# Two weight slabs in flight instead of three, and twelve places for gathered rows instead of eight

## What is computed

```python
s1 = jnp.einsum('thd,kd->thk', q[..., :half], keys_1)
s2 = jnp.einsum('thd,kd->thk', q[..., half:], keys_2)
...
act = jax.nn.gelu(jnp.einsum('td,tkd->tk', xt, peer_u[it]), approximate=False)
return jnp.einsum('tk,tkd->td', gt * act, peer_v[it])
```

## Time and profile before

| what | value |
|---|---|
| median of the 3 timed runs | 3032.58 us (3027.8 to 3038.06) |
| profiled execution, time | 3017.4 us |
| profiled execution, span from the first to the last instruction | 3016.1 us |
| PE busy | 2197.6 us, 73% |
| DVE busy | 1695.0 us, 56% |
| POOL busy | 1269.6 us, 42% |
| mean granted TensorE clock | 0.821 of full speed |
| moved by DMA | 829.54 MB, of it 539.99 MB gathered and 283.19 MB of slabs |

### The profile page before, as it was taken

How to read it: one execution, slowest core, us unless ns; L and a number is a source line. 1 busy time by engine, 2 the same in 40 slices (tenths; PEclk the granted TensorE clock), 3 DMA queues, 4 the chain that set the end, 5 groups by cost and what they waited for, 6 DMA issues and landing times. The chain is left out here.

```text
span 3016.1 us, 24315 instructions
## 1 busy us (share of the span) xinstructions
PE 2197.6 (73%) x8042; PEld 1333.1 (44%) x8042; DVE 1695.0 (56%) x3733; ACT 514.4 (17%) x1409; POOL 1269.6 (42%) x1041
## 2 busy tenths in 40 slices
PE   6997981155592594788682478979956598969988
PEld 3535861032342482433342247658423343436543
DVE  2512017968778767766577896765565854224200
ACT  1202000111210100122100452012001431004210
POOL 1000002466656666666666775664654633100000
PEclk9796996577595697899886558989978689988999
DMA  5210433698789899989889887999998879942466
GB/s 182 80 70 28 153 120 108 199 366 329 258 318 357 310 413 355 381 323 341 330 297 407 305 286 274 400 371 390 369 372 324 283 259 403 358 152 98 169 243 222
DMA packets 173485, 829.54 MB, mean 275 GB/s; under 512 B 20496, under 2 KB 21696, under 8 KB 155568
## 3 DMA queue, kind: packets, MB, share of 16 engines
q0 software_dynamic: 148464, 539.99, 48.9%
q1 hardware_dynamic: 21600, 283.19, 24.1%
q10 hardware_dynamic: 3296, 4.80, 0.5%
HBM read 825.81 MB, written 2.10 MB: 274 GB/s over the span
## 5 line engine op out<-in xcount | busy, mean ns | idle before, releaser
L326 POOL DMA_INDIRECT picks_rows<-peer_u_dram,expert x512 | 643.2, 1256 | 861.9 <-DVE expert L1545 481.2
L326 POOL DMA_INDIRECT picks_rows<-peer_v_dram,expert x512 | 618.5, 1208 | 479.5 <-DVE h L392 319.5
L386 DVE CUSTOM_DVE_ANT_0 picks_rows<-picks_rows,xn 128x1024 f32<-128x1024 f32 x512 | 611.5, 1222 | 184.5 <-DMA picks_rows<-peer_u_dram,expert 162.0
L392 DVE SCALAR_TENSOR_TENSOR h<-picks_rows,picks_weight,h 128x1024 f32<-128x1024 f32 x416 | 533.8, 1283 | 172.7 <-DMA picks_rows<-peer_v_dram,expert 98.2
L477 PE MATMUL psum<-weight_ring,hnT 128*128 128x512 f32 (+4 forms) x576 | 234.3, 568 | 15.5 <-DVE hnT L633 9.9
L1842 PE MATMUL psum<-weight_ring,aT 128*128 128x512 f32 x512 | 220.5, 593 | 2.3 <-ACT aT L2162 1.4
L415 PE MATMUL psum<-picks_rows,picks_diag 128*128 128x512 f32 x384 | 170.8, 605 | 19.1 <-ACT picks_diag L344 18.8
L477 PEld LDWEIGHTS psum<-weight_ring,hnT 128*128 128x128 f32 (+1 forms) x576 | 104.9, 184 | 143.8 <-issue 128.0
L1842 PEld LDWEIGHTS psum<-weight_ring,aT 128*128 128x128 f32 x512 | 97.0, 190 | 124.2 <-issue 121.0
L668 PE MATMUL psum<-identity_sb,n_scaled 128*128 128x128 f32 (+1 forms) x104 | 23.7, 408 | 157.1 <-DVE n_scaled L652 157.1
L477 PE MATMUL psum<-weight_ring,mergedT 128*128 128x512 f32 x256 | 115.9, 614 | 25.6 <-DVE mergedT L1267 24.2
(11 more groups left out here) (370 smaller groups left out, 2925.9 us busy)
## 6 DMA issues: line engine op xcount, KB each, us to landing
weight_ring<-slabs_dram SPq DMA_DIRECT2D x125, 2048.0 KB, 9.8
weight_ring<-slabs_dram SPq DMA_DIRECT2D x10, 1024.0 KB, 7.9
picks_rows<-peer_u_dram,expert POOLq DMA_INDIRECT x512, 7.2
picks_rows<-peer_v_dram,expert POOLq DMA_INDIRECT x512, 6.3
weight_ring<-slabs_dram SPq DMA_DIRECT2D x2, 1536.0 KB, 6.4
weight_ring<-slabs_dram SPq DMA_DIRECT2D x2, 1152.0 KB, 7.0
weight_ring<-slabs_dram SPq DMA_DIRECT2D x4, 576.0 KB, 5.9
weight_ring<-slabs_dram SPq DMA_DIRECT2D x4, 512.0 KB, 5.5
```

The source lines that it names most:

```text
L326: pool.indirect_dma_start(out=self.rows[:, n % GATHERS, :], out_offset=None, in_=table, in_offset=bass.IndirectOffsetOnAxis(ap=self.expert ...
L386: ins = nc.vector.tensor_tensor_reduce(out=row, in0=row, in1=self.x[t], scale=1.0, scalar=0.0, op0=ALU.mult, op1=ALU.add, accum_out=self.d ...
L392: ins = nc.vector.scalar_tensor_tensor(out=h, in0=row, scalar=self.weight[:, t % 2, k:k + 1], in1=h, op0=ALU.mult, op1=ALU.add)
```

## The change

The ring of weight slabs has two slabs instead of three, and its third slab's 16 KB per partition go to four more places for gathered rows, so that there are twelve. `cand_rest` no longer has memory of its own but lies in `scratch`.

```diff
-RING = 3
+RING = 2
 SLAB = KT * 512
...
-GATHERS = 8
+GATHERS = 12
 DIAGS = 8
...
         at_f = sb("at_f", [P, PH, 2, TOPK])
-        cand, cand_rest = sb("cand", [P, PH, N_SUMS]), sb("cand_rest", [P, PH, N_SUMS])
+        cand = sb("cand", [P, PH, N_SUMS])
+        cand_rest = scratch[:, 0:PH * N_SUMS].rearrange("p (h k) -> p h k", h=PH)
```

## The result

| | kernel before | changed kernel |
|---|---|---|
| median | 3030.93 us (3012.95 to 3042.47, 20 runs) | 3041.22 us (3026.99 to 3049.73, 20 runs) |
| span of the profiled execution | 3016.1 us | 3038.9 us |
| mean granted TensorE clock | 0.821 | 0.824 |

The ratio is 1.0038 [1.0025, 1.0051]: 11.5 us slower (7.6 to 15.5; the medians are 10.3 us apart), where +33 was forecast. The sign was right, the size was not. Repeated on a second chip the changed kernel stood at 1.0114 [1.0068, 1.0161], and on a third at 1.0035 [1.0015, 1.0054]. More on that under the last experiments.

The account below looks back on a forecast made before the run. DVE was taken as behind while picks run (502 to 2250 us), PE as the limit from 2250 us. Ring 78 us lost less places 45 gained is 33 more; scaled, 3032.6 x 1.011 = 3066 us, range 3005 to 3105.

Parts of the forecast that it names:

- "PE sets the pace" from 2250 us on: From 2250 us to the end PE is the limit, DVE and ACT only follow; the smaller ring costs most there.
- 38 - 7.4 + 23 = 54 us: Ring losses: 38 us from 2250 to 2650 us, 23 in the last run, without 7.4 at the compression.
- I count half, 14 us: Between 610 and 1950 us, two-tile runs: 28 us of slab waits on PE, half counted as loss, 14 us.
- The compression of the one-tile run: In the run from 2250 to 2650 us, first slab behind the branch gates: load 10.3 less cover 2.9, 7.4 us lost.
- "3 us" before 460 us: Three places behind 1024 KB slabs before 460 us, where PE is alone, about 1 us each: 3 us lost.
- The ring in all: Loss from two slabs instead of three, whole kernel: 3 + 14 + 38 + 23 = 78 us, between 50 and 110.
- The places: Gain from four more gathers under way or waiting, out of DVE's 260 us of waits: 45 us, bounds zero and 100.
- the stretch at a share of 0.97: 1050 to 1250 us, 46.0 us of DVE waits, DMA full: 8 us gained, only by what was filled ahead.
- the stretch from 1250: 1250 to 1500 us, 69.7 us of DVE waits at a DMA share of 0.90: 18 us gained.
- all outside the four rows: DVE waits outside the four listed stretches, 56 us in small pieces: 5 us gained.
- The clock "at nothing": New PE pauses of 1 to 7 us were taken to cost nothing through a lower PE clock afterwards.
- Rival C: Each PE pause also costs its clock, 2.5 us each: 34 us on the forecast, 3100 us; chance 0.15.

Follow-up runs that it names:

- the last experiments: The unedited changed kernel timed again on two other chips, against the kernel before: ratios 1.0114 and 1.0035 (3041.02 us).
- late2_g8: Kernel before (eight places, three slabs' memory), but slabs from 90 on take turns in two slots: 3095.54 us, ratio 1.0173.
- late_third: Changed kernel, but from pick 972 only eight places, the other four's memory being a third slab from slab 92 on: 2999.73 us, ratio 0.9848; again 0.9874.
- mid2_g8: Kernel before (eight places, three slabs' memory), but slabs 24 to 89 take turns in two slots: 3042.14 us, ratio 0.9996.
- both_third: As late_third, with the third slab for slabs 0 to 23 too: 3006.87 us, ratio 0.9899 to the kernel before; again 0.9862.
- early_back: Changed kernel, but twelve places only until pick 760, then eight, and the third slab back from slab 68 on: 2986.62 us, ratio 0.9868.

## Why the prediction was right in sign and wrong in size

- **"PE sets the pace" from 2250 us on, and each slab's price is landing less cover.** Right. 38 - 7.4 + 23 = 54 us forecast for the slabs from 90 on; late2_g8 lost 52 and late_third gave back 58. In the last run the waits of 4 to 5 us behind short slabs and 1.3 us between full ones are as worked out, and the loads of the last stretch land in 8.2 us, as in the earlier trace rows. The Trainium skill's fit beside the prices in the prediction (DMA: Bandwidth & Descriptors, anatomy of one DMA), 6.8 us for such a slab, is stated there for transfers that GpSimd issues. These loads come from SP, and the traces have 7.7 to 8.2 us.
- **"I count half, 14 us" for the waits between 610 and 1950 us.** This step failed. With the next one it makes up 21 of the 21.5 us by which the forecast was too high. The waits came (25.7 us, 22 of them new), but mid2_g8 shows their price as zero (its interval reaches to 5 us). The row beside which I counted half, PE's 16.99 us for `mergedT`, said it already: PE was early there by more than the merge's slabs could cost it.
- **The compression of the one-tile run, 7.4 of the 38 us.** The same fault. I took all behind 2250 us as bound by PE, but picks run on until about 2600, and the earlier trace rows has DVE at 203 of 400 us there. mid2_g8 holds this stall too (slabs 82 to 89), and nothing of it is in the time. The wait for `cmp_k_tok` right behind it, 21.9 us before and 3.1 in the changed kernel, was the place to look.
- **"3 us" before 460 us.** About right: 4 us by the profiles, 3.9 us of it waits. The 7.5 us in the table are measured from a quick profile. The timed runs cannot show so little: late_third and both_third do not differ.
- **The ring in all: 78, measured 62.** Without the 21 us that are hidden, and with 4 for 3 at the start, the sum is 58, within the 55 to 70 of the interval.
- **The places: 45, measured 50** (1.0206 to 1.0038), with 28 on the chip where the changed kernel stood at 1.0114. The size was right, its split was not. I gave 8 us to the stretch at a share of 0.97, because "nothing more can be moved" there: the waits fell by 30 us. That more was filled ahead than I allowed for is the likely reason; no run tests it by itself. I gave 18 to the stretch from 1250: its waits fell by 6. And I gave 5 to all outside the four rows: the waits there fell by 43. That the sum came out near 45 is luck.
- **The clock "at nothing".** Wrong by 1.5 to 2.7 us for each long pause, 8.0 us in the two late merges. It did not show as an excess: late2_g8's 52 us (44 to 61) hold the sum without it (54), the waits alone (49.2) and the waits with it (57). Rival C priced a pause well (2.5 us), but it counted ten of over 4 us in the one-tile runs, where there are six, one of them hidden. Its sign was blind: the granted clock from 2650 us on is a mean over the stretch and stayed at 0.93, though the slabs behind the pauses ran at 0.50 at first.
- **The base.** I scaled the sum by the median of the runs, which was right: the profile of the kernel before was a quick one.

Taken together: 33 - 21 (hidden) + 1 (start) - 5 (places) = 8, and 11.5 was measured, with an interval of 7.6 to 15.5. The places' 50 us are themselves a difference of two measured ratios, so the independent part of this sum is the ring's 58 for 62.

## What to carry to other kernels

A new wait costs only what is left of it after the next wait of the same engine for a slower one: before counting a share of it, look for that next wait and compare the two sizes, and let a partial version (the change in one stretch only) decide. Two uses of one piece of memory need not be traded for the whole run: here places for rows pay while VectorE is behind, a third slab where TensorE is, and sharing the memory in time (early_back, late_third, both_third) made of a change that costs 0.4% one that wins 1.0 to 1.5%. Single profiles of this kernel differ by 30 us in one stretch, so they show where time goes, and the timed ratios how much.

## What the runs showed of the hardware that I had not expected

- A pause of 4 to 6 us before a slab makes the slab's 16 matmuls take 8.7 to 9.9 us instead of 7.1, with a granted clock of 0.50 to 0.55 in their first 3.5 us; with five more products in the pause they take 7.13 at 1.00. Behind 3.6 us of pause, 64 matmuls took 15.6 for 14.0 us.
- PE stood without a visible reason for some 40 us in one profile, with single matmuls of 0.4 to 0.6 us between pauses of 1 to 2 us, and for shorter stretches in six others, the kernel before among them. A profile of the same program at the same DMA share of 1.02 had none. The cause is open.
- DVE's waits for gathers fell most where the DMA share was already 0.97 (46.0 to 16.1 us): a share of 0.97 there did not mean that the waits were throughput.
